# Second feed-forward product of a two-layer trunk: seven Strassen products over pairs of output tiles, k-tiles and token halves in place of eight

## What is computed

```python
def squared_relu_mlp(u, w1, w2):
    a = jax.nn.relu(u @ w1)
    return (a * a) @ w2
...
    for i in range(DEPTH):
        ...
        u = rms_norm(h, ffn_norm_g[i])
        h = h + squared_relu_mlp(u, ffn_w1[i], ffn_w2[i])
    return rms_norm(h[:, N_META:], final_norm_g)
```

## Time and profile before

| what | value |
|---|---|
| three runs | 1182.77, 1184.89, 1183.16 us |
| profiled execution, first to last instruction (span) | 1181.6 us; its own time isn't listed beside it |
| TensorE busy | 1158.5 us, 98% |
| VectorE busy | 589.3 us, 50% |
| ScalarE busy | 430.5 us, 36% |
| granted TensorE clock, mean | 0.996 of full speed |
| feed-forward of layer 0 | about 181 to 562 us |
| feed-forward of layer 1 | about 811 to 1170 us |

### The profile page before, as it was taken

How to read it: one execution, slowest core, us unless ns; L and a number is a source line. 1 busy time by engine, 2 the same in 40 slices (tenths; PEclk the granted TensorE clock), 3 DMA queues, 4 the chain that set the end, 5 groups by cost and what they waited for, 6 DMA issues and landing times.

```text
span 1181.6 us, 17931 instructions
## 1 busy us (share of the span) xinstructions
PE 1158.5 (98%) x7529; PEld 1056.3 (89%) x7529; DVE 589.3 (50%) x751; ACT 430.5 (36%) x634; POOL 2.3 (0%) x30
## 2 busy tenths in 40 slices
PE   6999999999998999999999999999999999999997
PEld 6999999999998999999999888787888888888886
DVE  5898896433432433445453345665533433433453
ACT  7437455312311321333343233543422322422432
POOL 0000000000000000000000000000000000000000
PEclk9999999999999999999999999999999999999999
DMA  6312023323232232323123212132332332322311
GB/s 204 101 71 72 1 79 100 107 72 108 72 108 73 72 108 77 103 80 100 37 72 91 89 36 72 36 108 72 107 106 73 108 98 80 106 88 89 107 37 72
DMA packets 98823, 100.20 MB, mean 85 GB/s; under 512 B 2786, under 2 KB 95644, under 8 KB 98748
## 3 DMA queue, kind: packets, MB, share of 16 engines
q1 hardware_dynamic: 98684, 99.02, 26.0%
q10 hardware_dynamic: 64, 0.07, 0.0%
HBM read 96.99 MB, written 2.10 MB: 84 GB/s over the span
## 4 chain that ended last, share of the span: by engine, by line
PE 96%; DVE 2%; DMA 1%; issue 1%; ACT 1%; SPq 0%; ACTq 0%; DVEq 0%
PE ps L1426 83%; PE ps L1637 5%; PE ps L1542 3%; PE ps L1679 1%; PE ps L1694 1%; PE ps L1474 1%; PE ps L1434 1%; DMA raw<-in_cp_w_in_dram 1%; DVE conv L1045 0%; DVE w_lo L423 0%; PE ps L1714 0%; PE ps L1705 0%; ACT w_hi L415 0%; DVE h L974 0%; DVE gated_lo L1314 0%
## 5 line engine op out<-in xcount | busy, mean ns | idle before, releaser
L415 ACT ACTIVATE w_hi<-raw 128x1024 fp32r<-128x1024 f32 x180 | 189.0, 1053 | 347.7 <-PE ps L1426 346.7
L1426 PE MATMUL ps<-u_lo,w_hi 128*128 128x272 f32 (+1 forms) x1120 | 299.8, 324 | 4.4 <-DVE u_lo L1002 2.7
L1426 PE MATMUL ps<-u_hi,w_lo 128*128 128x272 f32 (+1 forms) x1120 | 296.0, 320 | 2.3 <-issue 2.3
L1426 PE MATMUL ps<-u_hi,w_hi 128*128 128x272 f32 (+1 forms) x1120 | 296.0, 320 | 0.0
L423 DVE TENSOR_TENSOR w_lo<-raw,w_hi 128x1024 fp32r<-128x1024 f32 x180 | 220.1, 1225 | 108.4 <-ACT w_hi L415 108.4
L1426 PE MATMUL ps<-a_lo,w_hi 128*128 128x256 f32 (+2 forms) x912 | 234.8, 315 | 0.0
L1426 PE MATMUL ps<-a_hi,w_hi 128*128 128x256 f32 (+2 forms) x912 | 234.2, 314 | 0.0
L1426 PE MATMUL ps<-a_hi,w_lo 128*128 128x256 f32 (+2 forms) x912 | 234.0, 314 | 0.0
L1426 PEld LDWEIGHTS ps<-u_lo,w_hi 128*128 128x128 f32 x1120 | 184.5, 189 | 22.8 <-issue 7.7
L1426 PEld LDWEIGHTS ps<-u_hi,w_lo 128*128 128x128 f32 x1120 | 184.3, 189 | 17.8 <-issue 2.4
L1426 PEld LDWEIGHTS ps<-u_hi,w_hi 128*128 128x128 f32 x1120 | 185.3, 190 | 16.5 <-issue 1.2
(11 more groups left out here) (211 smaller groups left out, 866.6 us busy)
## 6 DMA issues: line engine op xcount, KB each, us to landing
raw<-in_ffn_w_dram SPq DMA_DIRECT2D x64, 1024.0 KB, 5.3
raw<-in_gla_w_in_dram SPq DMA_DIRECT2D x12, 1024.0 KB, 5.3
raw<-in_cp_w_in_dram SPq DMA_DIRECT2D x8, 512.0 KB, 5.4
raw<-in_cp_w_out_dram SPq DMA_DIRECT2D x4, 1024.0 KB, 5.1
raw<-in_gla_w_out_dram SPq DMA_DIRECT2D x4, 1024.0 KB, 5.0
xin<-in_x_dram SPq DMA_DIRECT2D x4, 512.0 KB, 5.2
raw<-in_cp_w_in_dram SPq DMA_DIRECT2D x2, 1024.0 KB, 5.0
out_dram<-y_tok SPq DMA_DIRECT2D x4, 512.0 KB, 3.0
```

The source lines that it names most:

```text
L415: act.activation(half_view(w_hi, n), half_view(raw, n), ACT.Copy).then_inc(w_hi_ready, 1)
L1426: last = mm(ps[:, n % NS, c:c + b - a], l, r[:, a - origin:b - origin], start=(k == 0 and i == 0), stop=(k == count - 1 and i == 2))
```

## The change

In blocks 0 to 2 of each layer, units 8 to 15 become four pairs. For a pair of output tiles (m), with the eight k-tiles taken as four even/odd couples and the tokens as two halves, the 2x2x2 product is made by seven products in Winograd's form. The weight side has A11, A12, A22 and four sums S1 to S4 (`pair_sums`, VectorE); the activation side has E1, E2, O1, O2 (even or odd tile, early or late tokens) and four differences T1 to T4. A product is 4 k-couples x 3 matmuls of half the tokens (264 columns in layer 0, 256 in layer 1). ScalarE copies partial results between PSUM banks (`z`, `low`) or to SBUF (`kept`), from where VectorE adds them to the late half of `h`. The weight groups of a pair are four: (A11, A12), (S1, S2), (S3, S4), (A22); each is split while the pair before runs, those of the first pair in units 4 to 7. `act2`, `a_hi`, `a_lo` are written in block 3 alone. SP's loop of loads is written out; weight halves outside the V and layer-0 output blocks lie contiguously (`w_view`), and `changed` gains two blocks.

```diff
+PAIRED = FBLK - 1
+HALF = TOK // 2
+E1, T1, T2, O1, O2, T3, T4, E2 = range(8)
+U_A11, U_A12, U_S1, U_S2, U_S3, U_S4, U_A22 = range(7)
+UNIT = KD // 2 * P
...
+GROUPS = [0]
+for _b in range(NB):
+    GROUPS.append(GROUPS[-1] + (4 if pair_block(_b) else 2))
+FB_GROUPS = GROUPS[B_F0 + 8] - GROUPS[B_F0]
...
-    changed = n // 2 in (B_OUTP, B_OUTP + 1, B_F0, B_F0 + 1)
+    changed = n // 2 in (B_OUTP, B_OUTP + 1, B_F0, B_F0 + 1, B_V, B_V + 1)
...
+            c_hi = sb("c_hi", [P, 7, KD // 2, HALF], F32R, paired)
+            c_lo = sb("c_lo", [P, 7, KD // 2, HALF], F32R, paired)
+            s_sum = sb("s_sum", [P, 4, KD // 2, P], F32, paired)
+            parts8 = sb("parts8", [P, 2, 8, HALF], F32, paired)
...
+        def w_view(t, n):
+
+            b, j = divmod(n, 2)
+            if B_OUTP <= b < B_F0 or B_V <= b < B_K:
+                return half_view(t, n)
+            return t[:, b % 2, KD * P * j:KD * P * (j + 1)].rearrange("p (k n) -> p k n", k=KD)
...
+        def pair_group_freed(eng, layer, fb, p, g, it):
+
+            if p < 0:
+                filled(eng, SLOT["ffn", layer, fb, KD // 2 + g], it)
+            elif g < 2:
+                eng.wait_ge(product_done, 5 * pair_number(layer, fb, p) + (4, 3)[g] + 20 * it)
+            else:
+                filled(eng, pair_slot(layer, fb, p) + g - 2, it)
...
+        def pair_group(layer, fb, p, g):
+
+            b = pair_raw(layer, fb, p)
+            src = (lambda: blocks_of(b, 0, 0, 2), lambda: s_sum[:, 0:2, :, :], lambda: s_sum[:, 2:4, :, :],
+                   lambda: blocks_of(b, 1, 1))[g]()
+            first, count = ((U_A11, 2), (U_S1, 2), (U_S3, 2), (U_A22, 1))[g]
+            return src, units_of(w_hi, first, count), units_of(w_lo, first, count)
+
+        def pair_hi(layer, fb, p, g, it=0):
+
+            act = nc.scalar
+            b = pair_raw(layer, fb, p)
+            if g in (1, 2):
+                act.wait_ge(s_ready, 4 * pair_number(layer, fb, p) + g + 2 + 16 * it)
+            else:
+                act.wait_ge(raw_loaded[b % 2], raw_count(b) + 64 * it)
+            pair_group_freed(act, layer, fb, p - 1, g, it)
+            src, hi, _ = pair_group(layer, fb, p, g)
+            act.activation(hi, src, ACT.Copy).then_inc(w_hi_ready, 1)
...
+            dve.wait_ge(raw_loaded[b % 2], raw_count(b) + 64 * it)
+            if p:
+                dve.wait_ge(w_lo_ready, GROUPS[b - 1] + 3 + FB_GROUPS * it)
+            elif fb:
+                dve.wait_ge(w_lo_ready, GROUPS[b - 5] + 3 + FB_GROUPS * it)
+            dve.tensor_tensor(s1, a21, a22, ALU.add).then_inc(s_ready, 1)
+            dve.tensor_tensor(s3, a11, a21, ALU.subtract).then_inc(s_ready, 1)
+            dve.wait_ge(s_ready, n + 1 + 16 * it)
+            dve.tensor_tensor(s2, s1, a11, ALU.subtract).then_inc(s_ready, 1)
+            dve.wait_ge(s_ready, n + 3 + 16 * it)
+            dve.tensor_tensor(s4, a12, s2, ALU.subtract).then_inc(s_ready, 1)
...
+            n, w = pair_slot(layer, fb, p), HALF if layer == 0 else SEQ // 2
+            bank = lambda s, i: ps[:, s % NS, BANK - w:BANK] if i == 0 else ps[:, s % NS, BANK:BANK + w]
+            return bank(n, 0), bank(n, 1), bank(n + 1, 0), bank(n + 1, 1)
...
-                with sp.Fori(0, FBLK) as fb:
+                for fb in range(FBLK):
+                    b = first + 8 * fb
                     for j in range(4):
-                        load(first + j, w1[:, :, bass.ds(fb * D + 256 * j, 256)], fb)
+                        load(b + j, w1[:, :, fb * D + 256 * j:fb * D + 256 * (j + 1)])
                     for j in range(4):
-                        load(first + 4 + j, w2[:, bass.ds(fb * KD, KD), 256 * j:256 * (j + 1)], fb)
+                        load(b + 4 + j, w2[:, fb * KD:(fb + 1) * KD, 256 * j:256 * (j + 1)])
...
+                    if i % 2 == 0:
+                        if count >= 2:
+                            act.wait_ge(part_lo_ready, 3 * (count - 1) + 12 * it)
+                        act.activation(now[:, E1::E2 - E1, :], src, ACT.Square).then_inc(sq_ready, 1)
+                        if i < KD // 2:
+                            split_hi(block + i + 4, it)
+                        else:
+                            pair_hi(layer, fb, 0, i - KD // 2, it)
+                        act.wait_ge(t_ready, 3 * count + 1 + 12 * it)
+                        act.activation(c_hi[:, E1:T1 + 1, j, 0:w], now[:, E1:T1 + 1, :], ACT.Copy)\
+                           .then_inc(part_hi_ready, 1)
+                    else:
+                        act.activation(now[:, O1:O2 + 1, :], src, ACT.Square).then_inc(sq_ready, 1)
+                        act.wait_ge(t_ready, 3 * count + 2 + 12 * it)
+                        act.activation(c_hi[:, T2:O2 + 1, j, 0:w], now[:, T2:O2 + 1, :], ACT.Copy)\
+                           .then_inc(part_hi_ready, 1)
+                        act.wait_ge(t_ready, 3 * count + 3 + 12 * it)
+                        act.activation(c_hi[:, T3:T4 + 1, j, 0:w], now[:, T3:T4 + 1, :], ACT.Copy)\
+                           .then_inc(part_hi_ready, 1)
+                        if i < KD // 2:
+                            split_hi(block + i + 4, it)
+                        else:
+                            pair_hi(layer, fb, 0, i - KD // 2, it)
+                for p in range(KD // 2):
+                    q = pair_number(layer, fb, p)
+                    z, y, low, x_bank = pair_parts(layer, fb, p)
+                    kept = act2[:, p % 2, 0:2 * w].rearrange("p (t n) -> p t n", t=2)
+
+                    def next_hi(g):
+                        if p < KD // 2 - 1:
+                            pair_hi(layer, fb, p + 1, g, it)
+                        else:
+                            split_hi(block + 16 + g, it)
+
+                    act.wait_ge(product_done, 5 * q + 1 + 20 * it)
+                    act.activation(z, x_bank, ACT.Copy).then_inc(seeded, 1)
+                    act.wait_ge(product_done, 5 * q + 2 + 20 * it)
+                    act.activation(kept[:, 1, :], y, ACT.Copy).then_inc(copied, 1)
+                    act.wait_ge(product_done, 5 * q + 3 + 20 * it)
+                    act.activation(kept[:, 0, :], x_bank, ACT.Copy).then_inc(copied, 1)
+                    next_hi(0)
+                    act.wait_ge(product_done, 5 * q + 5 + 20 * it)
+                    act.activation(low, x_bank, ACT.Copy).then_inc(seeded, 1)
+                    next_hi(1)
+                    next_hi(2)
+                    next_hi(3)
+
...
+                    def part_lo(first, last, n):
+                        dve.wait_ge(part_hi_ready, 3 * count + n + 12 * it)
+                        V.tensor_tensor(c_lo[:, first:last + 1, j, 0:w], now[:, first:last + 1, :],
+                                        c_hi[:, first:last + 1, j, 0:w].bitcast(F32), ALU.subtract)\
+                         .then_inc(part_lo_ready, 1)
+
+                    relu_out(layer, fb, i, tokens, it)
+                    if i % 2 == 0:
+                        if i < KD // 2:
+                            split_lo(block + i + 4, it)
+                        else:
+                            if i == KD // 2:
+                                pair_sums(layer, fb, 0, it)
+                            pair_lo(layer, fb, 0, i - KD // 2, it)
+                        dve.wait_ge(sq_ready, t + 1 + 8 * it)
+                        V.tensor_tensor(now[:, T1, :], now[:, E2, :], now[:, E1, :], ALU.subtract)\
+                         .then_inc(t_ready, 1)
+                        part_lo(E1, T1, 1)
+                    else:
+                        dve.wait_ge(sq_ready, t + 1 + 8 * it)
+                        V.tensor_tensor(now[:, T2, :], now[:, O2, :], now[:, T1, :], ALU.subtract)\
+                         .then_inc(t_ready, 1)
+                        V.tensor_tensor(now[:, T3, :], now[:, O2, :], now[:, E2, :], ALU.subtract)
+                        dve.wait_ge(t_ready, 3 * count + 2 + 12 * it)
+                        V.tensor_tensor(now[:, T4, :], now[:, O1, :], now[:, T2, :], ALU.subtract)\
+                         .then_inc(t_ready, 1)
+                        part_lo(T2, O2, 2)
+                        part_lo(T3, T4, 3)
+                        if i < KD // 2:
+                            split_lo(block + i + 4, it)
+                        else:
+                            pair_lo(layer, fb, 0, i - KD // 2, it)
+                for p in range(KD // 2):
+                    q = pair_number(layer, fb, p)
+                    n = pair_slot(layer, fb, p)
+                    kept = act2[:, p % 2, 0:2 * w].rearrange("p (t n) -> p t n", t=2)
...
+                    if p < KD // 2 - 1:
+                        pair_sums(layer, fb, p + 1, it)
+                    dve.wait_ge(copied, 2 * q + 2 + 8 * it)
+                    V.tensor_tensor(late, late, kept, ALU.add).then_inc(late_added, 1)
+                    next_lo(0)
+                    next_lo(1)
+                    dve.wait_ge(late_added, q + 1 + 4 * it)
+                    add_pair(0)
```

(38 more changed lines are left out.)

194 lines of the change are left out of this document (143 added, 51 removed).

## The result

The changed kernel takes **1163.47 us** (median of four, 1161.42 to 1164.85) beside 1183.22 us for the kernel before: ratio 0.9826, interval 0.9814 to 0.9839, so 19.8 us less. The forecast was 1167.5 us, with a range of 1160 to 1178.

What follows compares the result with a forecast made beforehand. TensorE's issue time was taken as the bound, busy 98%. Terms -31.6 + 14.0 + 0.6 + 1.3 = -15.7 us brought the 1181.6 us span to 1165.9, with 1.6 us around it 1167.5 us; range 1160 to 1178.

Steps and rivals of the forecast that it cites:

- TensorE's stream: Paired products in both layers: fewer or shorter matmuls take 31.6 us off TensorE's issue time, ends 31.0 and 32.1.
- The joints: First to second product, six times: TensorE waits for ScalarE's queued `z` copy, longer in block 0; 14.0 us added.
- restarts: TensorE starting again after each joint's stall: some 0.1 us each, 0.6 us in all.
- Rounds of VectorE: First product, relu to next relu in layer 0: 5.33 us even, 5.48 odd, 6.12 with sums, against TensorE's 5.87.
- Inside the pairs: VectorE and ScalarE work within each pair stays hidden behind TensorE, costed at nothing.
- the cover: Inside pairs, 0.8 us to spare before TensorE waits; rival that it is thin: 10 us, 1177 us, 11%.
- Boundary to V: Layer 0's end into the V projection: u_lo(7) comes late behind a weight split, 1.3 us once; 0 to 2.5.
- Back edges: Jumps back of both layers' TensorE loops: instruction refetching taken as unchanged, costed at nothing.
- one of the two ends: Layer 0's loop is now kept instead of fetched again: -4.0 us.
- The other end: Layer 1's loop is fetched again: +4.0 us; as a rival 1171 us, 12%.
- Layer 0's refetch gone: Rival at layer 0's jump back: its code is no longer fetched again; about 1161 us, 13% shared with half the stalls.
- half the stalls: Rival at the joints: only half their waiting appears; about 1161 us, 13% shared with layer 0's refetch gone.

Runs made afterwards that it cites:

- the run with four copies: Changed kernel with four further ScalarE copies of 128x528 ahead of the `z` copy of each pair but a block's first: 1171.13 us.
- three such reorderings: Changed kernel with first `z` copy ahead of T3/T4's hi copy and weight group 3, T1 ahead of the weight subtraction, `prep` and `rest_of_u` ahead of splits: 1148.83 us.
- the repetition: The changed kernel measured once more, with nothing altered: 1163.48 us, ratio 0.9832 to the kernel before.
- the run with T1 first: Changed kernel with VectorE's small difference T1 put ahead of the weight subtraction in even units: 1157.26 us, ratio 0.9773.
- the longest loop: Changed kernel with 512 further fulfilled TensorE waits in the body of layer 0's loop, 1746 instructions: 1187.16 us.
- the two shorter of the longer loops: Changed kernel with 128 or 256 further fulfilled TensorE waits in the body of layer 0's loop: 1163.82 us and 1161.02 us.

## Why the prediction was right, point by point

- **TensorE's stream, -31.6:** right, measured -32.8. Short matmuls cost in proportion: 9.93 us for 84 of 256 columns is 118.2 ns, the lower of the two starts shown in the earlier trace rows; I took the middle. In layer 0, 10.21 / 84 = 121.5 ns. The Trainium skill's sustained figures (TensorE: Matmul & The Clock Gate, "Back-to-back issue gap"), by which layer 1 would have lost time, are not borne out: 118 ns where they give some 98 at 256 columns, and 232 where they give 131 at 512.
- **The joints, +14.0, and restarts, +0.6:** right in place, number, cause and size: by starts 14.0 us in all, restarts included. A late block's joint costs 1.60 us (forecast 1.57 and 0.1), those of the two block 0s 3.17 and 4.43 (forecast 3.3 and 4.5). The idle time that the profile shows, 1.33 us each and 11.9 in all, is the smaller reading. S2 starts 4.42 us after the pair's first matmul (forecast 4.50); the `z` copy takes 0.37 us, not the 0.47 of a scaled copy to SBUF, which I had taken as the nearest row (unscaled copies of this shape to SBUF take 0.38 to 0.39). Relu(7) was late by 1.66 and 2.92 us (forecast 1.69 and 2.97). That the queue order sets the wait, and the reciprocal its excess, two runs show.
- **Rounds of VectorE:** 5.35 and 5.48 us, 6.04 with the sums (forecast 5.33, 5.48, 6.12), from durations by shape and the order of two queues alone.
- **Inside the pairs, 0:** right, no wait; the run with four copies shows that the cover has an end.
- **Boundary to V, +1.3:** measured 1.4 by starts, 1.2 of it shown as idle.
- **Back edges, 0:** this step was wrong. "1440 nearer the fetched, so I change nothing" measured nearness by length, and the loop of layer 0 was kept, one of the two ends. That end was also sized too small: -4.0 counts the two gaps alone, where the profiled execution of before lost 6.0 us with the clock behind them. The runs put place together with length in its stead; why one place costs a fetch and another doesn't stays open. The other end, +4.0 in layer 1, did not come.
- **Not costed at all:** the clock, after a long joint (0 to 3.4 us in the two profiles of the changed kernel) and between the feed-forwards (1.5 us more than in before's profile), and a later start-up, 0.5.

So the span was forecast at 1165.9 us and came out 6.3 lower: -1.2 (pairs), -0.6 (joints with restarts), -6.0 (jump), +0.1 (boundary), +1.5 (clock between the feed-forwards), +0.5 (start-up), and -0.6 that stays open. The median lies 2.1 us above this profiled execution, the fastest of the four, and with 0.2 more around the span that leaves the forecast of 1167.5 us 4.0 above the measurement. That it is only 4.0 is luck in part: the jump and the clock, both put at nothing, pulled in opposite directions. Layer 0's refetch gone was a rival (13%), and it is what happened. The prediction gave it with half the stalls as "about 1161"; by its own -4.0 it makes 1163.5, and that the median of 1163.47 meets this is chance, since the jump was worth more and the clock took it back.

## What to carry to other kernels

Where an engine hands over between two stages, read the waited-for engine's queue backwards from the instruction that releases it, and put that instruction ahead of work that is due later: three such reorderings, with no operation removed, were worth 14.6 us between the medians (12.2 by starts), three quarters of what the change itself gave. Small operations on which another engine's step depends belong ahead of a long one on their own queue. For a hardware loop near the size that is kept, count on neither outcome: the same body cost or saved 4 us by where it stood.

## What the runs showed that was not expected

- Eight profiled executions have a joint at which TensorE idled 1.9 us or more at a stretch. Behind such a joint the clock fell in five of them, in layer 1 or in both layers, and in three nowhere. In the three kernels whose joint waits are all at or under 1.44 us it stayed full at these places. But the idle stretch alone doesn't decide. The clock also fell behind the boundary's wait of 1.16 us, in the repetition and in the run with T1 first (its window below). It fell behind before's jump but not behind the gaps of 1.45 and 2.79 us of the longest loop. And it fell between the feed-forwards in every profile, with no idle time of TensorE in the 9 us before.

```profile
550.00:555.00 5.00, 5.00 (x29) 4.56 (x28) 1.34 (x3) 1.70 (x4) 0.00 (x0) 0.66 0.59 201
```

- Fulfilled waits cost TensorE nothing visible when 8 or 16 of their instructions stand in a row (the two shorter of the longer loops, with blocks of 89.3 us as in the changed kernel), and about 1.4 us when 32 do.
- Code ahead of a loop moves the loop's cost: 64 instructions without effect made a kernel 0.4% faster.
